# A scan's running sums spread over all rows by one rounded product instead of four exact ones

## What is computed

```
cum = jnp.cumsum(dtc * A, axis=1)              # running sum over the chunk's 128 tokens, per head
seg = cum[:, :, None] - cum[:, None, :]
decay = jnp.exp(jnp.where(causal, seg, -jnp.inf))
w = cb[..., None] * decay * dtc[:, None]
y = jnp.einsum('btsgk,bsgkp->btgkp', w, xc)
y = y + jnp.einsum('btgn,bgkpn->btgkp', cc, state) * jnp.exp(cum)[..., None]
```

## Time and profile before

| | |
|---|---|
| median of 3 runs | 2102.53 us (2102.21 to 2103.66) |
| profiled execution, its own time | 2102.39 us |
| its span | 2100.6 us |
| mean granted TensorE clock over the span | 0.991 of full |
| TensorE busy | 2036.5 us (97%) |
| VectorE busy | 1049.6 us (50%) |
| ScalarE busy | 966.4 us (46%) |
| GpSimd busy | 747.8 us (36%) |

### The profile page before, as it was taken

The page is one execution under the profiler, slowest core; times in us unless marked ns, Lnnn a source line. Parts: engine busy times, 40 slices in busy tenths (PEclk is TensorE's granted clock), DMA queues, the critical chain, the costliest instruction groups (busy, mean ns, idle before and its releaser), DMA issues.

```text
span 2100.6 us, 26382 instructions
## 1 busy us (share of the span) xinstructions
PE 2036.5 (97%) x10432; PEld 1693.6 (81%) x10432; DVE 1049.6 (50%) x1934; ACT 966.4 (46%) x1698; POOL 747.8 (36%) x341
## 2 busy tenths in 40 slices
PE   7999999999999999999989999999999999999997
PEld 6878888877778888888768888888888878888886
DVE  3364553367654566666445564422436574443214
ACT  4355444366644455454524544432355455444323
POOL 2422133333333322232233444444332234444442
PEclk9999999999999999999999999999999999999999
DMA  4211122211122222122122222333311122223332
GB/s 179 80 41 52 50 71 82 89 51 51 51 61 91 62 70 71 61 61 71 61 70 81 91 96 100 100 93 93 95 47 37 63 81 100 96 96 101 88 95 68
DMA packets 50059, 162.60 MB, mean 77 GB/s; under 512 B 5392, under 2 KB 12176, under 8 KB 49808
## 3 DMA queue, kind: packets, MB, share of 16 engines
q1 hardware_dynamic: 49504, 159.54, 24.0%
q10 hardware_dynamic: 432, 1.39, 0.2%
HBM read 158.80 MB, written 2.10 MB: 77 GB/s over the span
## 4 chain that ended last, share of the span: by engine, by line
PE 90%; DVE 6%; ACT 3%; issue 1%; DMA 0%; POOL 0%; SPq 0%; ACTq 0%; DVEq 0%
PE ps L1793 21%; PE ps L1796 21%; PE ps L1794 21%; PE ps L1843 3%; PE ps L1858 3%; PE ps L1805 2%; PE ps L1808 2%; PE ps L1806 2%; PE ps L1827 2%; PE ps L1851 2%; PE ps L1935 1%; PE ps L1925 1%; PE ps L1821 1%; PE ps L1818 1%; PE ps L1820 1%; PE ps L1837 1%
## 5 line engine op out<-in xcount | busy, mean ns | idle before, releaser
L2512 POOL TENSOR_TENSOR wl<-st,wh 128x1024 fp32r<-128x1024 f32 (+2 forms) x311 | 713.6, 2297 | 1268.0 <-ACT wh L1957 1267.7
L1957 ACT ACTIVATE wh<-st 128x1024 fp32r<-128x1024 f32 (+2 forms) x311 | 314.1, 1010 | 567.0 <-PE ps L1796 501.4
L1793 PE MATMUL ps<-xh,wh 128*128 128x512 f32 x1368 | 559.7, 409 | 0.0
L1796 PE MATMUL ps<-xh,wl 128*128 128x512 f32 x1368 | 534.7, 391 | 0.0
L1794 PE MATMUL ps<-xl,wh 128*128 128x512 f32 x1368 | 533.1, 390 | 0.0
L1796 PEld LDWEIGHTS ps<-xh,wl 128*128 128x128 f32 x1368 | 256.8, 188 | 56.4 <-POOL wl L2512 0.9
L1793 PEld LDWEIGHTS ps<-xh,wh 128*128 128x128 f32 x1368 | 257.3, 188 | 55.2 <-issue 8.9
L1794 PEld LDWEIGHTS ps<-xl,wh 128*128 128x128 f32 x1368 | 257.6, 188 | 52.1 <-issue 5.3
L2471 DVE SCALAR_TENSOR_TENSOR tmp<-ps,vec,tmp 128x510 f32<-128x510 f32 (+1 forms) x176 | 131.3, 749 | 222.7 <-ACT tmp L2127 219.7
L2429 DVE SCALAR_TENSOR_TENSOR res<-res,ps 128x512 f32<-128x512 f32 (+1 forms) x37 | 22.5, 613 | 217.5 <-PE ps L1796 209.9
L1793 PE MATMUL ps<-fa_h,wh 128*128 128x512 f32 x308 | 122.4, 397 | 0.0
(11 more groups left out here) (275 smaller groups left out, 3656.0 us busy)
## 6 DMA issues: line engine op xcount, KB each, us to landing
st<-in_f_up SPq DMA_DIRECT2D x88, 512.0 KB, 3.2
st<-in_s_xbc SPq DMA_DIRECT2D x32, 512.0 KB, 3.5
st<-in_f_dn SPq DMA_DIRECT2D x32, 512.0 KB, 3.5
st<-in_o_fm SPq DMA_DIRECT2D x24, 512.0 KB, 3.5
st<-in_e_fm SPq DMA_DIRECT2D x21, 512.0 KB, 3.5
st<-in_s_z SPq DMA_DIRECT2D x16, 512.0 KB, 3.5
st<-in_s_out SPq DMA_DIRECT2D x16, 512.0 KB, 3.6
st<-in_f_dn SPq DMA_DIRECT2D x16, 384.0 KB, 3.1
```

The costliest lines, as they stand in the source:

```text
L1793: e.matmul(u.bank.ap, hi, x.h[:, kk, :], start=first, stop=False)
L1796: e.matmul(u.bank.ap, lo, x.h[:, kk, :], start=False, stop=last).then_inc(S["mm"], 1)
L1957: e.activation(P.mem["wh"][w.m % NWR][:, 0:w.n], P.mem["stage"][w.m % NSTAGE][:, 0:w.n], ACT.Copy).then_inc(S["w_hi"], 1)
L2512: e.tensor_tensor(P.mem["wl"][w.m % NWR][:, 0:w.n], P.mem["stage"][w.m % NSTAGE][:, 0:w.n], P.mem["wh"][w.m % NWR][:, 0:w.n].bitcast(F32), ...
```

## The change

Once, in `decay`, the running sums of all 32 heads are also made with the heads on the partitions: `cum_t`, four matmuls with `dta` of a chunk as the stationary operand (128 rows, 32 columns) and the triangle as the moving one. ScalarE rounds the result into the upper 32 rows of `s_ct` (`ct_hi`), VectorE puts what is left into the next 32 rows (`ct_lo`), and ScalarE copies a selection table (`sel`), 32 new columns of the constants. Both new tiles lie over the two rope tables, which are not used in this stage. A head's `cum_b` is then one matmul of 512 columns: the head's column of the selection table, repeated 128 times, over 64 rows, with `s_ct`. The planner's lengths are given anew: 240 ns for `cum_b` in place of 896, 900 for `cum_t`, 210 for `sel`.

```diff
-C_N = 1990
+C_SEL = 1990
+C_N = 2022
...
-           "cb": 896, "cum_b": 896, "y_mm": 1580, "w_hi": 1048, "table": 1283, "conv0": 778, "f0": 778, "ln": 680,
+           "cb": 896, "cum_b": 240, "cum_t": 900, "sel": 210, "y_mm": 1580, "w_hi": 1048, "table": 1283, "conv0": 778, "f0": 778, "ln": 680,
...
         dec["cum"] = yield ("cum_n", cum, cb, t)
+        ctb = yield from P.taken(P.at)
+        t = yield ("cum_t", ctb, dta, dec["dta"])
+        ct = mem["s_ct"]
+        t = yield ("ct_hi", ct[0:32, :], ctb.ap[0:32, :], t, P.rope_used)
+        t = yield ("ct_lo", ct[32:64, :], ctb.ap[0:32, :], ct[0:32, :], t)
+        ctb.release(t)
+        dec["ct"] = [t, (yield ("sel", mem["s_sel"][0:64, :], P.c(C_SEL, 32)[0:64, :], P.rope_used))]
         t2 = yield ("wend_a", wend, cb, cum, dec["cum"])
...
-            t = yield ("cum_b", cbc, dta, h, tdta)
+            t = yield ("cum_b", cbc, mem["s_sel"][0:64, h:h + 1], mem["s_ct"][0:64, :], dec["ct"])
...
-        elif kind == "cum_b":
-            bank, dta, h, ready = o
+        elif kind == "cum_t":
+            bank, dta, ready = o
             pe.freed(bank)
             pe.wait_ge(ready)
             for c in range(4):
-                t = e.matmul(cols(bank.ap, c), dta[:, c, h:h + 1].to_broadcast([128, 128]), P.c(C_TRI),
-                             start=True, stop=True, skip_group_check=True)
-            t.then_inc(S["cum_b"], 1)
+                t = e.matmul(bank.ap[0:32, c * 128:(c + 1) * 128], dta[:, c, :], P.c(C_TRI), start=True, stop=True,
+                             skip_group_check=True)
+            t.then_inc(S["cum_t"], 1)
+        elif kind == "cum_b":
+            bank, sel, ct, ready = o
+            pe.freed(bank)
+            pe.wait_ge(ready)
+            e.matmul(bank.ap, sel.to_broadcast([64, 128]), ct, start=True, stop=True).then_inc(S["cum_b"], 1)
...
+            e.activation(ct, bank, ACT.Copy).then_inc(S["ct_hi"], 1)
...
+            e.tensor_tensor(lo, bank, hi.bitcast(F32), ALU.subtract).then_inc(S["ct_lo"], 1)
...
+        mem["s_ct"] = at("s_ct", o + 4 * C_SIN, [128, 512], F32R)
+        mem["s_sel"] = at("s_sel", o + 4 * C_COS, [128, 32], F32R)
...
+    c[:, C_SEL:C_SEL + 32] = (p[:, None] % 32 == np.arange(32)[None, :])
```

More of the change, by code:

```diff
@@ L65 @@
     "pe": ("mm", "mm_half", "mm_tok", "ones", "blk", "perm", "score", "flip", "pv", "feat", "va_t", "dt_t", "cumsum",
-           "bc_t", "x_t", "cb", "u_mm", "cum_b", "y_mm"),
+           "bc_t", "x_t", "cb", "u_mm", "cum_t", "cum_b", "y_mm"),
     "act": ("w_hi", "table", "sq", "ln", "rs", "split_hi", "gate", "va_in", "qsq", "exp", "sink", "flip_a",
             "sub_sq", "lam_e", "conv0", "z_in", "xsilu", "zsilu", "bt", "u_in", "cc_e", "sg_e", "dt_in", "dt_abs",
-            "dt_e", "dt_ln", "a_exp", "wend_e", "gsq", "gln", "grs", "msq", "ln_out", "ln_hi", "csq",
+            "dt_e", "dt_ln", "a_exp", "ct_hi", "sel", "wend_e", "gsq", "gln", "grs", "msq", "ln_out", "ln_hi", "csq",
             "f0", "fsilu", "sine", "lat", "q_in", "v_a", "head_hi", "gate_in", "gate_s"),
@@ L73 @@
             "lam_m", "lam_r", "lam_d", "lam_o", "sub_g", "sub_e", "sub_a", "rec2", "mix_c", "mix_d", "tap", "xs",
-            "cbm", "seg", "seg_m", "st0", "st", "cc_m", "y_d", "y_z", "gadd", "gnrm", "dt_b", "dt_o", "dta", "cum_n",
+            "cbm", "seg", "seg_m", "st0", "st", "cc_m", "y_d", "y_z", "gadd", "gnrm", "dt_b", "dt_o", "dta", "cum_n", "ct_lo",
             "wend_a", "wend_m", "x8", "res_al", "var", "ln_cen", "ln_mul", "ln_lo", "cen", "shift", "first", "ftap",
@@ L1305, in scan @@
             yield lambda: None not in G.x_t and "wend" in dec and not (g and None in got[g - 1].z_t)
-        tc, tw, tdt, tdta = dec["cum"], dec["wend"], dec["dt"], dec["dta"]
+        tc, tw, tdt = dec["cum"], dec["wend"], dec["dt"]
         P.put("table", "silu_and_others", [])
@@ L2080, in act_program @@
             e.activation(out, out, ACT.Ln, bias=1.0).then_inc(S["dt_ln"], 1)
+        elif kind == "ct_hi":
+            ct, bank, ready, freed = o
+            act.wait_ge(ready)
+            act.wait_ge(freed)
+            e.activation(ct, bank, ACT.Copy).then_inc(S["ct_hi"], 1)
+        elif kind == "sel":
+            out, src, freed = o
+            act.wait_ge(freed)
+            e.activation(out, src, ACT.Copy).then_inc(S["sel"], 1)
         elif kind == "a_exp":
@@ L2410, in dve_program @@
                             ALU.mult).then_inc(S["cum_n"], 1)
+        elif kind == "ct_lo":
+            lo, bank, hi, rounded = o
+            dve.wait_ge(rounded)
+            e.tensor_tensor(lo, bank, hi.bitcast(F32), ALU.subtract).then_inc(S["ct_lo"], 1)
         elif kind == "wend_a":
```

## The result

| | before | after |
|---|---|---|
| median | 2103.1 us (4 runs, 2102.21 to 2105.53) | 2085.1 us (4 runs, 2082.07 to 2090.41) |
| profiled execution, its own time | 2102.39 us | 2086.61 us |
| its span | 2100.6 us | 2084.7 us |
| mean granted clock over the span | 0.991 | 0.988 |

The ratio is 0.9918, with a 95% interval of 0.9906 to 0.993. That is 17 us by the ratio, 18 us between the two medians and 15.9 us between the two spans. The forecast was 2087 us. The sum came out, but not all of its terms did, and a part of the gain was made where nothing of the change is computed.

What follows compares the result with a forecast made beforehand. TensorE was taken to bound the middle of the scan, ScalarE and VectorE its end. Seven groups 15.8 us, less 1.2 for cum_t, plus 0.6 for the eighth group, gave 15.2 off 2102.39: 2087 us, range 2081 to 2094 (83%).

Steps and rivals of the forecast that it cites:

- What bounds the kernel: Mid-scan: a microsecond less on TensorE saves one if VectorE and ScalarE keep up; the stage's end is another matter.
- The products: Each scan group: three heads' cum_b 1.03 us instead of 2.68, the fourth gains 0.61; 2.26 us a group.
- The change of form: Around the new 64*128 products: entering or leaving another form costs TensorE time, 0.34 us both ways for three heads.
- no cost of form: Rival, 25%: changing form around the new products costs nothing, 2.74 us gained a group, 2083.5 us in all.
- not hidden: Rival, 14%: each new product pays its operand load of 0.19 us, 5.3 us less gain, 2092.5 us.
- `cum_t`: Right after cumsum: adds 1.2 us on TensorE once; ct_hi, ct_lo and sel behind it cost nothing.
- The margin of 0.6 us: In a scan group, VectorE's product ends 0.6 us before the first y_mm; this margin shouldn't close.
- the order turns against TensorE: Rival, 12%: heads wait in y_mm for VectorE or ScalarE; the gain is gone at 0.54 us a head.
- The eighth group: Last scan group, chain on ScalarE and VectorE: gain between 0 and 2.3 us, taken as 0.6.
- The stages behind the scan change by no more than 1 us.: Behind the scan: a length change over 1 us would show the prediction wrong, as only the planner's starting point is touched.
- at most 0.13 us: Kernel start: the constants' load grows by 32 columns in 1990, costing at most this; taken as nothing.
- The other two signs of being wrong: In the scan stage: TensorE idle in the middle of the stage, or a y_mm waiting for VectorE.

Runs made afterwards that it cites:

- e3: The changed kernel with the new product over all 128 rows, the lower 64 zeroed once: 2085.24 us, ratio 0.9923.
- e10: The changed kernel with the product over 128 rows and GpSimd's w_lo cut in four: 2063.89 us, ratio 0.9808.
- e5: The changed kernel with GpSimd's w_lo cut into four instructions: 2067.83 us, ratio 0.9834.
- e4: The changed kernel with the planner's length of cum_b put back to 896 ns: 2100.34 us, ratio 0.9989.
- e9: The kernel before with 128 unused bytes behind the constants and w_lo cut in four, without the new product: 2085.07 us, ratio 0.9905.
- e1: The kernel before with 128 unused bytes per partition behind the constants, nothing else changed: 2095.71 us, ratio 0.997.
- e2: The changed kernel with 384 more bytes behind the constants, arrays again 128 past a multiple of 256: 2094.38 us, ratio 0.9962.
- e8: The changed kernel with 256 more bytes behind the constants: 2090.53 us in one run.
- e11: The changed kernel with the product over 128 rows and w_lo cut in two: 2080.13 us, ratio 0.9883.

## Why the prediction was right, point by point

**What bounds the kernel.** Right for the kernel before: TensorE in the middle, other engines at the end. Wrong was the sentence that a microsecond less on TensorE is one less of time as long as the others "keep up", judged by shares of 61% and 64%. VectorE's share in the middle is 65% after, against 64% forecast and with the time of the holds in it, and still it sets the time for 15 us of each group.

**The products.** Right. Form 64\*128, loads hidden, 1.10 us for three (1.03) and 0.74 for the fourth (0.79). With place and holds out of it a group gains 2.32 us (2.26).

**The change of form.** Right in kind: the gaps are there and go when the form is the same (e3). In the chain it costs 0.35 us a group (e10 against e5), not 0.48. The rival *no cost of form* fell.

**The loads.** The rival *not hidden* fell: the three products take 0.89 us with their exit, and none pays 0.19.

**`cum_t`.** Right: from where the projection behind 663.79 was due, 664.02, to 665.22 (665.45 − 0.23 for the next one) it is 1.20 us. `ct_hi` (0.59), `ct_lo` (0.68) and `sel` (0.21) cost nothing.

**The margin of 0.6 us.** This step failed: "the margin shouldn't close". It closed in the six middle groups, at the third `y_mm`, for 0.32 us, because GpSimd held the split `sy_l` ahead of it for 1.9 us in each; with short holds (e5) the wait is gone. GpSimd was in no term of the prediction. With the 0.02 by which the products were dearer together (1.84 against 1.82) that is nearly all of the 0.36 us a group that are missing, 2.1 us over six groups. I had checked the group's first `y_mm` and not the others. Group 0 gave 0.70 us less than forecast; there too a copy is held (1.93 us at 702.31) ahead of the last `y_mm`, but I have not taken that group apart. The rival *the order turns against TensorE* was real in mechanism, and far from its turning point of 0.54 us a head; with the old length (e4) it comes to 16.7 us of waits and leaves almost no gain.

**The eighth group.** Mis-sized, and in both directions. With short holds it gives 1.95 us of the possible 2.3 (e9, e5), since less of the chain stands on long VectorE instructions than I thought: they were held, not long. In the changed kernel two such holds cost 2.74 us and a stretch of low clock from 1027.6 to 1031.0 us followed them, in which `y_mm`'s steps took 0.42 us instead of 0.22. Forecast +0.6, result −0.36.

**"The stages behind the scan change by no more than 1 us."** Failed by its own test: 4.9 us. What I costed at "at most 0.13 us" was the load of 32 more constants; their place in memory was no term of the sum at all, and it was worth 7 to 9 us. The other two signs of being wrong came up as well: TensorE was idle for 0.9 of the middle 300 us, and a `y_mm` waited for VectorE in each of the middle groups.

So the forecast of 2087 against 2085.1 us is right in the mechanism of the product and in its largest term. That it is so close is partly luck: 3.8 us less in the scan and 0.45 before it, against 4.9 us more behind it, which the product did not make.

What stays open: why the low clock's stretches differ between the kernels, by 8.6 us behind the scan; and why arrays at odd multiples of 128 bytes are read more slowly. The runs show that they are, and for matmuls of 512 columns only.

## What to carry to other kernels

Check every meeting of two engines in the period that you shorten, not only the first; and read an instruction that is recorded far longer than its like as a held one, and look at what GpSimd does at that time. Where GpSimd has time to spare, cut its long instructions in pieces. When a change moves arrays, undo the move alone before you credit the change: here it made 7 to 9 of the 17 us.

## What the runs showed of the hardware

- A rounded matmul of 512 columns takes 227 to 228 ns start to start if its moving operand lies in arrays that begin at a multiple of 256 bytes in the partition, and 232 to 233 ns at 128 past one, 2% more (e1, e2, e8). With 256 columns no difference was seen.
- GpSimd's subtraction of 1024 columns (2.3 us) stops VectorE's copies, updates and products from SBUF until it ends, in the scan for up to 2.0 us beyond their own time. Instructions that read PSUM ran beside it at their usual 0.26 us (L2363 from 738.33 us on, with GpSimd at work from 738.25 to 740.65). Cut in four pieces of 742 ns mean it holds VectorE for some 0.2 to 0.6 us in most places, and the kernel takes 17 us less (e5). Over 128 rows the cut in four gains 21 us and the cut in two 5 (e3, e10, e11).
- A wait of 2.74 us, with TensorE busy for 4.26 us of the 7 around it, was followed by 3.4 us at the lower clock level (the changed kernel).
